# Four weight tiles part by part behind each norm, in a float32 transformer step on one core

## The reference

```python
x = x + 0.5 * mod[2] * swiglu(modulated_norm(x, norm_ffn1, mod[0], mod[1]), w_ffn1_in, w_ffn1_out)
h = modulated_norm(x, norm_mix, mod[3], mod[4])     # rmsnorm(x, gain) * (1 + scale) + shift
x = x + mod[5] * mixer(h)                           # h @ w_in, then DeltaNet and attention, then @ w_out
x = x + 0.5 * mod[8] * swiglu(modulated_norm(x, norm_ffn2, mod[6], mod[7]), w_ffn2_in, w_ffn2_out)
y = rmsnorm(x, norm_final)                          # mod = silu(cond) @ w_ada + b_ada, 9 x 1024 columns
```

## Time and profile before

| | us |
|---|---|
| median of 3 runs | 1831.31 |
| lowest, highest | 1827.92, 1831.51 |
| span of the profiled execution, first to last instruction | 1824.8 |
| TensorE busy | 1692.8 (93%) |
| VectorE busy | 1013.0 (56%) |
| ScalarE busy | 476.5 (26%) |
| GpSimd busy | 263.7 (14%) |
| mean granted TensorE clock | 0.946 of full |

### The profile page before, as it was taken

How to read it: one execution, slowest core, us unless ns; L and a number is a source line. 1 busy time by engine, 2 the same in 40 slices (tenths; PEclk the granted TensorE clock), 3 DMA queues, 4 the chain that set the end, 5 groups by cost and what they waited for, 6 DMA issues and landing times.

```text
span 1824.8 us, 28725 instructions
## 1 busy us (share of the span) xinstructions
PE 1692.8 (93%) x11299; PEld 1618.8 (89%) x11299; DVE 1013.0 (56%) x1765; ACT 476.5 (26%) x824; POOL 263.7 (14%) x213
## 2 busy tenths in 40 slices
PE   6799999999996999989878999888979999999997
PEld 5799999999996998866668888788979999999997
DVE  5766666664536764856647887678452332222223
ACT  4322222221213333324541110112232222221112
POOL 1200000000003000010026665663030000000000
PEclk9799999999997999996889999869979999999999
DMA  8344444453322221210000000000212222222221
GB/s 269 100 142 138 138 138 138 138 161 103 122 86 81 70 81 47 58 59 0 1 6 1 1 1 1 21 10 1 81 35 80 70 71 78 76 73 81 70 78 72
DMA packets 187755, 135.90 MB, mean 74 GB/s; under 512 B 8176, under 2 KB 173349, under 8 KB 187557
## 3 DMA queue, kind: packets, MB, share of 16 engines
q1 hardware_dynamic: 164981, 112.39, 20.4%
q10 hardware_dynamic: 22704, 22.55, 4.1%
HBM read 131.51 MB, written 3.41 MB: 74 GB/s over the span
## 4 chain that ended last, share of the span: by engine, by line
PE 79%; DVE 15%; ACT 3%; issue 2%; DMA 0%; POOL 0%; DVEq 0%; SPq 0%; ACTq 0%
PE ps L1341 20%; PE ps L1343 20%; PE ps L1342 20%; PE ps L1711 3%; PE ps L1715 2%; PE ps L1599 2%; PE ps L1388 1%; DVE h_lo L807 1%; PE ps L1757 1%; PE ps L1620 1%; PE ps L1691 1%; DVE r_s L1137 1%; DVE conv_acc L956 1%; DVE h_hi L806 1%; DVE att_s L1039 1%
## 5 line engine op out<-in xcount | busy, mean ns | idle before, releaser
L1341 PE MATMUL ps<-h_hi,w_lo 128*128 128x320 f32 x1920 | 607.1, 316 | 39.0 <-DVE h_lo L807 32.0
L1342 PE MATMUL ps<-h_lo,w_hi 128*128 128x320 f32 x1920 | 599.7, 312 | 0.0
L1343 PE MATMUL ps<-h_hi,w_hi 128*128 128x320 f32 x1920 | 599.5, 312 | 0.0
L777 DVE TENSOR_TENSOR w_lo<-w_raw,w_hi 128x1024 fp32r<-128x1024 f32 x168 | 206.1, 1228 | 391.1 <-ACT w_hi L483 389.6
L1341 PEld LDWEIGHTS ps<-h_hi,w_lo 128*128 128x128 f32 x1920 | 366.7, 191 | 46.4 <-issue 21.8
L1342 PEld LDWEIGHTS ps<-h_lo,w_hi 128*128 128x128 f32 x1920 | 367.1, 191 | 1.0 <-issue 0.7
L1343 PEld LDWEIGHTS ps<-h_hi,w_hi 128*128 128x128 f32 x1920 | 366.4, 191 | 0.0
L483 ACT CAST w_hi<-w_raw 128x1024 fp32r<-128x1024 f32 x168 | 175.4, 1045 | 290.6 <-PE ps L1343 227.6
L1341 PE MATMUL ps<-act_hi,w_lo 128*128 (+1 forms) x704 | 218.0, 310 | 0.0
L1343 PE MATMUL ps<-act_hi,w_hi 128*128 (+1 forms) x704 | 217.7, 309 | 0.0
L1342 PE MATMUL ps<-act_lo,w_hi 128*128 (+1 forms) x704 | 217.7, 309 | 0.0
(11 more groups left out here) (277 smaller groups left out, 2088.3 us busy)
## 6 DMA issues: line engine op xcount, KB each, us to landing
w_raw<-in_w_ffn_in SPq DMA_DIRECT2D x88, 512.0 KB, 3.9
w_raw<-in_w_ffn_out SPq DMA_DIRECT2D x44, 512.0 KB, 3.6
ada_ffn<-in_w_ada ACTq DMA_DIRECT2D x43, 512.0 KB, 3.7
w_raw<-in_w_in SPq DMA_DIRECT2D x28, 512.0 KB, 3.8
ada_ffn<-in_w_ada SPq DMA_DIRECT2D x13, 512.0 KB, 3.5
ada_tile<-in_w_ada SPq DMA_DIRECT2D x10, 512.0 KB, 7.7
w_raw<-in_w_out SPq DMA_DIRECT2D x8, 512.0 KB, 4.1
ada_wide<-in_w_ada SPq DMA_DIRECT2D x3, 1024.0 KB, 8.6
```

The lines of the kernel that those rows point to most:

```text
L777: nc.vector.tensor_tensor(w_lo[s][:], w_raw[s][:], w_hi[s][:].bitcast(F32), ALU.subtract)\
L1341: nc.tensor.matmul(out, lo, xh, start=start, stop=False)
L1342: nc.tensor.matmul(out, hi, xl, start=False, stop=False)
L1343: return nc.tensor.matmul(out, hi, xh, start=False, stop=stop)
```

## The change

Behind each norm the first four weight tiles are multiplied together: for each part of h, PE does the six matmuls of tile 0, then of tiles 1, 2 and 3, into PSUM banks 0,1 to 6,7 (`first_four`). For that there are four more pairs of `w_hi` and `w_lo`, laid into the tail of `act_lo`, and the four tiles are loaded and split before the modulation on ACT's and DVE's queues; tiles 4 and 5 are split between parts of the modulation. EPS becomes the bias of the root, so ACT reads the mean from PSUM itself; the spreading matmuls become five transposes; part 0 is multiplied by `rstd` on DVE and no longer on POOL. The convolutions of tiles 0 to 7 are unrolled (two before), the FFN's first four pairs too. One adaLN pair moves from the hidden stage to the down projection. Cut to its core:

```diff
+def w_slot(i):
+    return i if i < 6 else i % 2
...
+            tails = [act_tail[:, NJ * T - (i + 1) * D:NJ * T - i * D] for i in range(8)]
...
+            w_hi += tails[0::2]
+            w_lo += tails[1::2]
... SP
-                for k in range(2):
-                    w_load(base + k, k, wi[:, :, k * DFF:k * DFF + P], first=(f == 0))
+                for i in range(4):
+                    w_load(base + i, i % 2, wi[:, :, ...], first=(f == 0 and i < 2))
... ACT
+            def w_high_at(base, i):
+                n = base + i
+                act.wait_ge(w_landed[n % 2], n * 8 + (16 - 8 * (n % 2)))
+                if i >= 6:
+                    act.wait_ge(tile_done, base + (i - 5 if i < 8 else i - 1))
+                elif base > 0:
+                    act.wait_ge(tile_done, n - 1 if i < 2 else base)
+                nc.scalar.copy(w_hi[w_slot(i)], w_raw[n % 2][:]).then_inc(w_hi_ready, 1)
...
             def norm(seq, spread=True):
-                act.wait_ge(var_ready, seq + 1)
-                nc.scalar.activation(tok_rs[:, 0:NT], tok_rs[:, 0:NT], ACT.Sqrt).then_inc(sd_ready, 1)
+                act.wait_ge(mean_mm, seq + 1)
+                nc.scalar.activation(tok_rs[:, 0:NT], ps[:, 0, 0:NT], ACT.Sqrt, bias=eps_col[:]).then_inc(sd_ready, 1)
... modulate on ACT, after part k
+                    if k in (3, 5):
+                        w_high_at(base, 4 + (k - 3) // 2)
... norm 0 on ACT
             norm(0)
-            w_high(0, 0, first=True)
+            for i in range(4):
+                w_high_at(0, i)
             act.wait_ge(ada_used, ADA_PE)
... norm 1 on ACT (norm 2 alike)
             norm(1)
-            modulate(1)
+            for i in range(1, 4):
+                w_high_at(TILE_WIN, i)
+            modulate(1, TILE_WIN)
...
+            def to_conv(m, k, first=False):
+                if first and m in (5, 6):
+                    w_high_at(TILE_WIN, m + 1)
+                if not first:
+                    w_high(m + (TILE_WIN + 1), 1 - k)
                 act.wait_ge(tile_done, m + (TILE_WIN + 1))
...
+            to_conv(0, 0, True)
+            for m in range(1, 6):
+                to_conv(m, m % 2, True)
+                from_conv(m - 1, 1 - m % 2)
+            to_conv(6, 0, True)
+            from_conv(5, 1)
+            to_conv(7, 1)
+            from_conv(6, 0)
+            with act.Fori(0, 2) as i:
... DVE
-                dve.wait_ge(mean_mm, seq + 1)
-                nc.vector.tensor_scalar(tok_rs[:, 0:NT], ps[:, 0, 0:NT], EPS, None, ALU.add).then_inc(var_ready, 1)
...
+                dve.wait_ge(rstd_ready, seq + 1)
+                nc.vector.tensor_tensor(scratch[0][:], x_t[:, 0, :], rstd[:], ALU.mult).then_inc(hn_first, 1)
... modulate on DVE, after part k
+                    if k in (4, 6):
+                        w_low_at(base, 4 + (k - 4) // 2)
... norm 1 on DVE (norm 2 alike)
+            for i in range(1, 4):
+                w_low_at(TILE_WIN, i)
+            modulate(1, TILE_WIN, 1)
...
+            def conv(m, k, first=False):
+                if first and m in (5, 6):
+                    w_low_at(TILE_WIN, m + 1)
+                if not first:
+                    w_low(m + (TILE_WIN + 1), 1 - k)
                 dve.wait_ge(proj_out, m + 1)
...
+            for m in range(7):
+                conv(m, m % 2, True)
+            conv(7, 1)
+            with dve.Fori(0, 2) as i:
... POOL
-                for k in range(KD):
+                for k in range(1, KD):
... PE
+            def first_four(base, nth):
+                for k in range(KD):
+                    pe.wait_ge(h_ready, nth * 8 + k + 1)
+                    for m in range(4):
+                        if k == 0:
+                            pe.wait_ge(w_lo_ready, base + m + 1)
+                        w = (w_hi[m][:, k * P:(k + 1) * P], w_lo[m][:, k * P:(k + 1) * P])
+                        for half in range(2):
+                            x = [h[k // 4][:, k % 4, half * HT:half * HT + HT] for h in (h_hi, h_lo)]
+                            ins = product(ps[:, 2 * m + half, 0:HT], k, w, x, k == 0, k == KD - 1)
+                        if k == KD - 1:
+                            ins.then_inc(tile_done, 1)
... spread_rs
+                    ins = nc.tensor.transpose(ps[:, 2 + t // 4, (t % 4) * P:(t % 4 + 1) * P],
+                                              tok_rs[:, t:t + 1].broadcast_to([P, P]), ident[:])
... behind norm 1
-            dense(0, 0, 8).then_inc(tile_done, 1)
+            first_four(TILE_WIN, 1)
+            for m in range(4, 8):
+                pe.wait_ge(w_lo_ready, TILE_WIN + m + 1)
+                pe.wait_ge(proj_out, m - 3 if m < 6 else m - 1)
+                dense(w_slot(m), 2 * (m % 2)).then_inc(tile_done, 1)
```

More of the change, by code:

```diff
@@ L182, in hybrid_step @@
             spare = [[holder(s)(f"spare{i}{c}", [P, 4, P]) for c in range(2)] for i in range(4)]
[L183 to L184 removed]
+        w_hi = [sb(f"w_hi{i}", [P, D], F32R)[:] for i in range(2)]
+        w_lo = [sb(f"w_lo{i}", [P, D], F32R)[:] for i in range(2)]
         with ExitStack() as s:
@@ L527, in hidden @@
                                          ACT.Silu).then_inc(silu_ready, 1)
-                    w_high(j * 2 + (base + 2), 0)
+                    if first and j >= 2:
+                        w_high_at(base, 2 * j + 2)
+                    if not first:
+                        w_high(j * 2 + (base + 2), 0)
                     act.wait_ge(act_ready, j + (J + 1))
                     nc.scalar.copy(pick(act_hi, j), act_f[par][:]).then_inc(acthi_ready, 1)
[L531 to L536, removed]
+                    if f == 0 and not (first and j == 1):
+                        ada_load(act, j + 1 if first and j == 0 else j, 0)
+                for j in range(4):
+                    hidden(j, j % 2, True)
+                with act.Fori(0, NJ // 2 - 2) as i:
                     for k in range(2):
-                        hidden(i * 2 + (2 + k), k, False)
+                        hidden(i * 2 + (4 + k), k, False)
                 for hf in range(2):
@@ L772, in _, with w_low_at @@
             own = Chain(dve, dve_own)
+            def w_low_at(base, i):
+                n = base + i
+                dve.wait_ge(w_hi_ready, n + 1)
+                nc.vector.tensor_tensor(w_lo[w_slot(i)], w_raw[n % 2][:], w_hi[w_slot(i)].bitcast(F32), ALU.subtract)\
+                    .then_inc(w_lo_ready, 1)
             def w_low(n, s):
@@ L853, in hidden @@
                 def hidden(j, par, first=False):
[L854 to L861, removed]
+                    for i in {2: (6,), 3: (7, 8)}.get(j, ()) if first else ():
+                        w_low_at(base, i)
+                    if not first:
+                        w_low(j * 2 + (base + 1), 1)
+                        w_low(j * 2 + (base + 2), 0)
+                    a = j if first and j == 0 else j - 1
+                    if f == 0 and not (first and j == 1):
+                        if not (first and j == 0):
+                            dve.wait_ge(ada_summed, j + (ADA_DVE - 1))
+                        ada_part(a, 0, ada_acc)
+                        ada_part(a, 1, ada_acc, range(4, 6))
                     dve.wait_ge(tile_done, j * 2 + (base + 2))
-                    if f == 0 and not first:
-                        mods_of(j - 1, 4 * par + 2, 1)
+                    if f == 0 and not (first and j < 2):
+                        mods_of(j - 2, 4 * par + 2, 1)
                     dve.wait_ge(silu_ready, j + (J + 1))
@@ L867, in hidden @@
                                             ps[:, 4 * par + 2:4 * par + 4, 0:HT], ALU.mult).then_inc(act_ready, 1)
-                    if f == 0:
-                        ada_part(j, 1, ada_acc, range(6, 8))
+                    if f == 0 and not (first and j == 1):
+                        ada_part(a, 1, ada_acc, range(6, 8))
                     dve.wait_ge(acthi_ready, j + (J + 1))
@@ L935, in _ @@
             ada_setup(2)
-            w_low(0, 0)
+            for i in range(4):
+                w_low_at(0, i)
             dve.wait_ge(cols_ready, 2)
@@ L941, in _ @@
                                              spread(cols_a[:, 0:2 * KD], 2), ALU.add))
-            modulate(0)
+            modulate(0, 0, 0)
             ffn(0)
             norm(1)
-            modulate(1)
-            def conv(m, k):
-                w_low(m + (TILE_WIN + 1), 1 - k)
+            for i in range(1, 4):
+                w_low_at(TILE_WIN, i)
[3 more added lines that the diff above has]
+                    w_low_at(TILE_WIN, m + 1)
+                if not first:
+                    w_low(m + (TILE_WIN + 1), 1 - k)
                 dve.wait_ge(proj_out, m + 1)
@@ L960, in conv @@
                 ins.then_inc(conv_ready, 1)
-            conv(0, 0)
-            conv(1, 1)
-            with dve.Fori(0, 5) as i:
+            for m in range(7):
+                conv(m, m % 2, True)
+            conv(7, 1)
+            with dve.Fori(0, 2) as i:
```

(8 more changed lines are left out.)

143 lines of the change are left out of this document (69 added, 74 removed).

## The result

| us | before | after |
|---|---|---|
| median of the runs | 1831.31 | 1838.37 |
| lowest, highest (5 runs each) | 1827.92, 1832.9 | 1837.2, 1839.36 |
| ratio of the runs, 95% interval | | 1.0042, 1.003 to 1.0053 |
| span of the profiled execution | 1824.8 | 1835.4 |

The kernel became slower by 7.7 us (5.5 to 9.7 by the interval), where 1830.3 was forecast, with a range up to 1837.5. The two profiled spans differ by 10.6 us, more than the runs do; this has to be kept in mind when the traces are laid side by side. On record a run's time lies about 2 us above its own span. So of the 6.5 us between the span before and the median before, some 4.5 are not what lies outside the span: the profiled execution was a quick one.

The account below looks back on a forecast made before the run. The prediction took PE as the bound (79% of the chain), waiting 32.0 us for `h_lo` behind norms. Terms -3.9, -2.4, -0.2 and +5.5 summed to -1.0 us from 1831.3: 1830.3, no change, range 1823.5 to 1837.5.

Parts of the forecast that it names:

- Norm 0: First norm: part 0 at 58.7 us, tile 3 done at 88.7 where it was 93.5; gain 3.9 us.
- price of four tiles: First four tiles behind a norm: 192 matmuls, 28.0 us, plus 2.0 for half clock; tile 3 ends 30.0 us behind part 0.
- Norm 1: Norm ahead of the mixer: tile 3 1.6 us better, then PE stalls 6.3 us for tile 6's split; net loss 5.5 us.
- upper bound: Split of tile 1 on DVE: the 1.2 us that `h_lo` loses beside POOL, making it 0.7 us later than taken.
- Norm 2 and the last norm: Norm 2: tile 3 at 1370.4 us, before 1372.90, gain 2.4; last norm: the missing add saves 0.2 us.
- The slower one: Rival: the fourth tile's load lands 1.9 us late at all three norms, +5.7 us, 1836.0; chance of this side 0.28.
- The faster one: Rival: tile 6 of w_in isn't late, tile 7 ends at 635.7, sum -9.4 us, 1821.9; chance of this side 0.27.

Follow-up runs that it names:

- e6: The kernel before with only one unused 4-byte column allocated, moving every buffer behind it by 32 bytes; 1830.54 us, ratio 1.0012.
- e7: The changed kernel with the ones and EPS columns in one allocation, so later addresses are those of the kernel before; 1836.09 us, ratio 1.0038.
- e8: Changed kernel, old layout, tiles 2 and 3 split behind part 0, tiles 0 and 1 before norm 0's adaLN copy, 6 to 12 across convolutions; 1804.65 us, ratio 0.9871.

## Why the prediction was wrong

**The mechanisms were right in the main, the balance was not.** The prediction's list of signs had a later part 0, one wait for `h_lo` at each norm, a wait of about 6 us for `w_lo` with a restart at half clock, and no gaps between parts. All of it is in the trace. The sum of -1.0 us should have been +5.5 by the same terms, and by the runs +7.7.

**Norm 0, -3.9 forecast, -0.3 measured.** This is the step that failed most. The forecast put part 0 at 58.7; it came at 61.0. It took the first weight load's time from the trace of before, as if nothing in the change touched it, and e6 shows that the added column did. With the old layout (e7) it came at 59.3. In the changed kernel `w_lo` of tile 1 ended at 47.6 instead of 45.9, which is 1.7 of the 2.3 us; behind the rest stands the load of the fourth tile, issued then, which landed 4.7 us later where 3.9 were taken. Then the price of four tiles: tile 1 released DVE at 90.60, tile 3 is 12 matmuls behind, 92.3, so 31.3 us after part 0 and not 30.0. The half clock lasted longer than the 3.3 and 5.2 us of the earlier trace rows:

```profile
61.00:64.00 3.00, 2.92 (x11) 2.92 (x12) 2.97 (x3) 1.20 (x2) 3.00 (x2) 0.50 1.08 291
64.00:68.00 4.00, 4.00 (x19) 4.00 (x18) 3.87 (x5) 3.02 (x5) 1.95 (x2) 0.59 0.01 2
68.00:72.00 4.00, 4.00 (x29) 4.00 (x28) 3.97 (x3) 2.36 (x4) 3.83 (x3) 1.00 0.00 0
```

These rows of the changed kernel (columns as above) lose 1.5 and 1.6 us to the clock, 3.1 together, where 2.0 were taken. 2.3 us of later start and 1.3 of price are the 3.6 that the term missed by.

**Norm 1, +5.5 forecast, +6.9 measured (7.1 at tile 7).** Part 0 came 1.1 us late, and not by `w_low` of tile 1: that took 1.72 us beside POOL, the price the forecast had as its upper bound, but began earlier and ended at 566.17, 0.4 us ahead of the forecast. It was the load of the fourth tile, issued then, which landed after 5.4 us instead of 3.9. Everything behind shifted with it; `w_lo` of tile 6 was done at 629.3 instead of 628.0. The wait was 6.3 us, as forecast, and PE then ran 4.4 us at half clock:

```profile
622.80:629.30 6.50, 0.30 (x3) 0.04 (x1) 6.32 (x9) 3.54 (x9) 0.00 (x0) 0.83 0.00 0
629.40:633.80 4.40, 4.40 (x16) 4.40 (x17) 4.26 (x6) 0.60 (x1) 0.00 (x0) 0.50 0.43 123
```

**Norm 2 and the last norm, -2.6 forecast, -1.1 measured.** From the mean to part 0 the forecast had 16.5 us, the trace has 16.3. But the mean itself, ten matmuls, took 2.29 us at half clock in this execution and 1.42 us at a granted clock of 0.85 in that of before (`L1440` and `L1360`; it took 1.28 to 2.29 us in the variants of before, so this part is chance), and tile 3 ended 30.7 us after part 0 instead of 30.0. The five transposes took 1.33 us, the value taken. By the Trainium skill ("TensorE: Matmul & The Clock Gate", Terms), four times faster than six plain pieces at 2.93 us would be about 0.6; the trace doesn't bear that out, it is 0.27 us a piece for 0.49, both at half clock.

**The rivals.** The slower one gave nearly the measured time, 1836.0, and that is in part luck: its cause acted, but with less than half its price. It had the fourth tile's load 1.9 us late at each norm, 5.7 in all. The load landed 4.7, 5.4 and 3.9 us after its issue at norms 0, 1 and 2, so it was 0.8, 1.5 and 0 late, 2.3 in all; at norm 2 it was issued when `w_lo` 1 ended at 1341.6 and split from 1345.64. The rest came from the layout, the half clock and the mean. What both sides overlooked is beside it: not only that this load could be slow, but that the whole of it need not stand in front of part 0. The faster one, that tile 6 isn't late, is refuted by the wait of 6.3 us; e8 shows that it comes true once the order of the queues is changed. The forecast treated the order as given and priced it to within 2 us at norm 1.

**The chance.** The three terms missed by 3.6, 1.4 and 1.5 us, all to the same side. Each gain was a difference of two large numbers (28 us of matmuls less 7 us of delay), with the load, the half clock and the first weight load taken at or near their favourable values. The range reached 1837.5 and should have reached 1840.

## What to carry to other kernels

When matmuls are regrouped to cover a slow supply, put the first item of the supply ahead of the extra preparation on every in-order queue: the four tiles together were worth about 8 us at norms 0 and 2, and the splits and loads ahead of part 0 took 7 to 8 us back at each norm until two of them were moved behind it. Results that come out in a bunch leave a backlog on the next engine, so whatever that engine prepares for the matmuls must be placed ahead of the backlog, with each later item too, or the stall moves on by one. A load that stands on the chain is priced where it stands, not by the median of all: 3.9 us held at norm 2, while norms 0 and 1 had 4.7 and 5.4. And after adding even a 4-byte buffer, compare the addresses of the others.

## What the runs showed of the hardware

- Moving all later buffers from multiples of 64 bytes to 32 past them slowed the adaLN loads into them: 1.74 us instead of 1.45 to issue one of 1 MB (e6, e7), 8.6 to 9.1 us instead of 7.2 to 7.7 for one of 512 KB. Loads into `w_raw`, which lies ahead of the new buffer, took 3.8 and 3.9 us in both. Only this one shift was tried, and not which part of the path is slower. The Trainium skill ("SBUF — State Buffer", Operand start alignment) says of such addresses only that they are legal, and that its runs timed nothing.
- A stretch of 845 matmuls with many short gaps took between 140.6 and 148.3 us in unchanged code, at granted clocks of 0.82 to 0.87 that don't order the lengths, against a spread of 1.3 us in the dense stretch from norm 2 to the end (six profiles of the kernel before and its variants). One profile of each kernel can therefore mislead by several us, and did here (10.6 us of span for 7.7 us of time).
